# A hybrid encoder layer on one core: the experts' turn shifted into the next mixing, and the scores of the expert search taken from one merged matrix

## The reference, cut to what matters

```python
proj = rms_norm(x) @ w_in                              # 1024 -> 2592 columns
y_r  = rwkv7_group(...)                                # recurrence with a state, prompt tiles in order
y_a  = swa_group(...)                                  # window attention over 256 keys
x    = x + concat(y_r, y_a) @ w_out
t    = rms_norm(x)
q    = (t @ w_q).reshape(T, 8, 2, 128)                 # 2048 columns
s1   = q[:, :, 0] @ key1.T;  s2 = q[:, :, 1] @ key2.T  # 16 blocks of 128 scores
# top 16 of each, top 16 of their sums: 8 x 16 = 128 experts for each token, gate = softmax
act  = gelu(down[expert] . t);   x = x + sum(gate * act * up[expert])
y    = rms_norm(x)
```

## Time and profile before

| | us |
|---|---|
| median of 3 runs | 4369.31 (4369.14 to 4375.14) |
| the profiled execution | 4367.83 |
| its span in the trace | 4365.9 |
| `project` | 0 to 335 |
| sample tile | 335 to 645 |
| eight turns | 645 to 4030, 422 each |
| experts of the last tile alone | 4030 to 4366 |

### The profile page before, as it was taken

The page is one execution under the profiler, slowest core; times in us unless marked ns, Lnnn a source line. Parts: engine busy times, 40 slices in busy tenths (PEclk is TensorE's granted clock), DMA queues, the critical chain, the costliest instruction groups (busy, mean ns, idle before and its releaser), DMA issues.

```text
span 4365.9 us, 47921 instructions
## 1 busy us (share of the span) xinstructions
PE 3366.5 (77%) x13668; PEld 1870.5 (43%) x13668; DVE 2944.6 (67%) x6184; ACT 1441.0 (33%) x4151; POOL 1366.7 (31%) x1160
## 2 busy tenths in 40 slices
PE   9996837886877697869776977787778777876656
PEld 5554534452545253526352635254435434552222
DVE  1003356758876877687767877786777687769765
ACT  1001203432443335233523352335233423342222
POOL 0000002434333334334333433343334343434443
PEclk9997668898889898979897989888878898898778
DMA  4102228989899989989998999899889988999998
GB/s 189 51 37 80 81 78 337 388 360 371 326 390 369 367 329 405 352 334 363 383 359 332 366 396 363 323 370 403 350 324 364 403 342 331 380 396 347 405 420 358
DMA packets 228898, 1410.30 MB, mean 323 GB/s; under 512 B 34211, under 2 KB 40739, under 8 KB 77654
## 3 DMA queue, kind: packets, MB, share of 16 engines
q0 software_dynamic: 165888, 1208.03, 69.9%
q1 hardware_dynamic: 60102, 181.96, 11.1%
q10 hardware_dynamic: 2592, 16.66, 0.9%
HBM read 1387.39 MB, written 20.41 MB: 322 GB/s over the span
## 4 chain that ended last, share of the span: by engine, by line
PE 31%; DVE 27%; DMA 12%; issue 9%; ACT 6%; DVEq 0%; POOL 0%; ACTq 0%; POOLq 0%; SPq 0%; PEldq 0%
PE mx_ps L1435 14%; DVE ex_rows L1462 10%; DMA ex_rows<-experts,ex_expert_c 8%; PE mx_ps L1185 4%; DMA mx_fac<-w_q 2%; PE mx_ps L1168 2%; DVE mx_pqb L1285 1%; DVE mx_fac L1286 1%; DVE mx_pqb L1283 1%; DVE ex_x2c L1472 1%; PE mx_ps L978 1%; PE mx_ps L974 1%; PE mx_ps L971 1%; ACT ex_diag L1416 1%; ACT ex_coef L1409 1%
## 5 line engine op out<-in xcount | busy, mean ns | idle before, releaser
L1397 POOL DMA_INDIRECT ex_rows<-experts,ex_expert_c x1152 | 1361.9, 1182 | 2970.3 <-PE mx_ps L1435 1339.0
L1435 PE MATMUL mx_ps<-ex_rows,ex_diag 128*128 128x512 f32 x3168 | 1772.9, 707 | 638.3 <-ACT ex_diag L1416 627.9
L1462 DVE CUSTOM_DVE_ANT_0 ex_rows<-ex_rows,ex_tnc 128x1024 f32<-128x1024 f32 x1152 | 1376.4, 1222 | 277.2 <-DMA ex_rows<-experts,ex_expert_c 255.4
L1435 PEld LDWEIGHTS mx_ps<-ex_rows,ex_diag 128*128 128x128 f32 x3168 | 662.0, 222 | 1559.2 <-issue 898.6
L1406 ACT ACTIVATE ex_coef<-ex_coef 128x1 f32<-128x1 f32 x1152 | 224.9, 202 | 1510.1 <-DVE ex_coef L1462 1508.0
L1472 DVE SCALAR_TENSOR_TENSOR ex_x2c<-ex_rows,ex_coef,ex_x2c 128x1024 f32<-128x1024 f32 x360 | 462.5, 1285 | 140.2 <-ACT ex_coef L1409 139.4
L1416 ACT ACTIVATE ex_diag<-cn_ident,ex_coef 128x128 f32<-128x128 f32 x792 | 294.5, 397 | 18.5
L260 PE MATMUL psP<-pj_w_in_sb,pj_hT 128*128 128x432 f32 x768 | 279.6, 526 | 0.0
L1409 ACT ACTIVATE ex_coef<-ex_coef,ex_gate_c 128x1 f32<-128x1 f32 x1152 | 277.1, 282 | 4.7
L229 DVE TENSOR_SCALAR pj_proj_sb<-psP,pj_rstd_a 128x432 f32<-128x432 f32 x27 | 18.0, 668 | 279.2 <-PE psP L260 244.9
L1406 ACT ACT_TABLE_LOAD x137 | 175.8, 1283 | 90.3 <-issue 55.2
(11 more groups left out here) (297 smaller groups left out, 3999.8 us busy)
## 6 DMA issues: line engine op xcount, KB each, us to landing
mx_fac<-w_q SPq DMA_DIRECT2D x54, 512.0 KB, 11.0
mx_ex<-w_out SPq DMA_DIRECT2D x36, 512.0 KB, 10.7
mx_ex<-w_q SPq DMA_DIRECT2D x36, 512.0 KB, 13.3
ex_rows<-experts,ex_expert_c POOLq DMA_INDIRECT x1152, 9.2
mx_p_cur<-w_q SPq DMA_DIRECT2D x27, 512.0 KB, 13.0
mx_xs<-w_q SPq DMA_DIRECT2D x27, 512.0 KB, 13.1
proj_rows<-pj_proj_sb ACTq DMA_DIRECT2D x9, 1296.0 KB, 4.7
mx_p_cur<-proj_rows SPq DMA_DIRECT2D x9, 1296.0 KB, 8.5
```

Source lines behind the costliest of these rows:

```text
L1397: pool.indirect_dma_start(rows[:, s % RING, :], None, A["experts"], bass.IndirectOffsetOnAxis(expert_c[:, s:s + 1], 0))\
L1435: last = pe.matmul(bank(6 + c), diag[:, n % DIAGS, :], up[:, r, c * 512:(c + 1) * 512], start=n == 0, stop=n == len(ON_PE) - 1)
L1462: dve.tensor_tensor_reduce(out=down[:, r, :], in0=down[:, r, :], in1=tnc[:, :], scale=1.0, scalar=0.0, op0=ALU.mult, op1=ALU.add, accum_ou ...
```

## The change

Five things are edited together.

1. **Written-out tiles.** The loops `Fori` over the eight turns become Python loops, so each engine's program holds all turns one after the other.
2. **The experts' turn is shifted.** The work on a tile's experts begins at mark 6 of the mixing (`BEGIN`) and ends at mark 75 (`END`), where marks 72 to 75 are marks 1 to 4 of the next mixing. A `Turn` object calls the old tile's work for marks 1 to 5 and its `finish` (final norm) at mark 6. The copies for the new tile come at mark 6 (`first`). After the last turn, `alone` works off the last tile's experts one slot a mark. `STAGES` has new numbers.
3. **Earlier loads.** `mix_sync` waits for the use of the last weight block (`w_used`) instead of `tile_end`. `mu` moves to `ex`, `k_a` to `arT`, `y_out` to `pqk`, and SyncE stores `y` between `mix_sync` and `route_sync`.
4. **One matrix of scores.** `w_sc` = `w_q` times the keys (1024 x 2048) is computed once on the device, in the first block while the samples are mixed: 32 parts of four products through one bank (`merge_tensor`), copied by ScalarE (`merge_scalar`), written to memory by SyncE (`merge_sync`). `Merge.upto` issues three parts for every two marks, up to mark 22.
5. **Routing.** PE multiplies `tn` (stationary) with 16 blocks of `w_sc` in products of 512 columns and gets the scores; two copies of 1024 columns take the place of eight of 512.

```diff
-STAGES = ((7, 13, 0.3), (16, 20, 0.5), (25, 18, 0.4), (28, 6, 0.1), (38, 20, 0.3),
-          (42, 6, 0.7), (48, 9, 0.8), (59, 17, 0.0), (67, 13, 0.0), (71, 6, 0.3))
+BEGIN, END = 6, MARKS + 4
+STAGES = ((7, 3, 0.3), (16, 21, 0.5), (25, 18, 0.4), (28, 7, 0.1), (38, 22, 0.3), (42, 7, 0.7),
+          (48, 11, 0.8), (59, 16, 0.0), (67, 12, 0.0), (71, 2, 0.3), (END, 9, 0.3))
...
+class Turn:
+    def upto(self, mark):
         while self.mark < mark:
             self.mark += 1
+            if self.ahead and self.mark < BEGIN:
+                self.ahead.upto(MARKS + self.mark)
+            if self.ahead and self.mark == BEGIN:
+                self.ahead.finish()
+            self.experts.upto(self.mark)
...
+class Merge:
+    def upto(self, mark):
+        end = max(self.done, min(32, mark * 3 // 2))
+        self.run(range(self.done, end))
+        self.done = end
...
             if not sample:
-                sp.wait_ge(tile_end.sem, tile_end.due(t, 0))
+                sp.wait_ge(w_used.sem, w_used.due(t, 0))
             sp.dma_start(p_cur[:, :], proj[bass.ds(P + src, P), :]).then_inc(p_in.sem, 16)
...
-            for g in range(4):
-                slots.upto(44 + g)
-                for j in range(4):
-                    w = weights(KC + 4 * g + j).rearrange("p (k n) -> p k n", n=P)
-                    for k in range(KC):
-                        last = pe.matmul(ps[:, 2 + g, j * P:(j + 1) * P], w[:, k, :], aT[:, k, :],
+            for side in range(2):
+                for k in range(KC):
+                    if k % 2 == 0:
+                        slots.upto(44 + (KC * side + k) // 4)
+                    w = weights(KC + KC * side + k)
+                    for n in range(2):
+                        last = pe.matmul(bank(2 + 2 * side + n), aT[:, k, :], w[:, n * 512:(n + 1) * 512],
                                          start=k == 0, stop=k == KC - 1)
                     last.then_inc(w_used.sem, 1)
...
-                for j in range(4):
-                    last = pe.matmul(ps[:, g, j * P:(j + 1) * P], s12[:, 4 * g + j, :], keysT[:, j % 2, :],
-                                     start=True, stop=True)
...
+            def merge_sync(sp):
+                for j in range(4):
+                    sp.dma_start(wqT[:, j, :], A["w_qT"][j]).then_inc(wq_in[j].sem, 16)
+                for i in range(32):
+                    j, side = i // 2, i % 2
+                    sp.wait_ge(merge_copied.sem, i + 1)
+                    sp.dma_start(A["w_sc"].rearrange("(k p) n -> p k n", p=P)[:, 4 * side:4 * side + 4, j * P:(j + 1) * P],
+                                 merged[:, i % 4, :, :]).then_inc(merge_stored[i % 4].sem, 16)
+                    if side and j + 4 < 16:
+                        sp.wait_ge(merge_out.sem, i + 1)
+                        sp.dma_start(wqT[:, j % 4, :], A["w_qT"][j + 4]).then_inc(wq_in[j % 4].sem, 16)
...
+            def merge_tensor(pe):
+                def products(parts):
+                    for i in parts:
+                        j, side = i // 2, i % 2
+                        pe.wait_ge(wq_in[j % 4].sem, 16 * (j // 4 + 1))
+                        if i:
+                            pe.wait_ge(merge_copied.sem, i)
+                        for k in range(4):
+                            at = (4 * side + k) * P
+                            last = pe.matmul(ps[:, 7, k * P:(k + 1) * P], wqT[:, j % 4, at:at + P], keysT[:, j % 2, :],
...
-                with dve.Fori(0, T) as t:
-                    slots = experts_vector(dve, t)
+                ahead = None
+                for t in range(T):
+                    experts = experts_vector(dve, t)
+                    slots = Turn(ahead, experts)
                     dve.wait_ge(tile_end.sem, tile_end.due(t + 1, 0))
                     mix_vector(dve, t + 1, m, slots)
                     route_vector(dve, t + 1, slots)
                     dve.sem_inc(tile_end.sem, 1)
-                    hand_over(dve, t + 1, slots)
-                    slots.finish()
-                experts_vector(dve, T).finish()
+                    hand_over(dve, t + 1)
+                    slots.upto(MARKS)
+                    ahead = experts
+                ahead.finish()
+                experts_vector(dve, T).alone()
```

More of the change, by code:

```diff
@@ L324, in stage_tables @@
     for s in range(SLOTS):
-        mark = min(next(m for m, n in enumerate(upto) if n > s) + ADD_LAG, MARKS)
+        mark = min(next(m for m, n in enumerate(upto) if n > s) + ADD_LAG, END)
         owed += share[mark]
@@ L357, in finish, with alone, __init__, upto @@
     def finish(self):
-        self.upto(MARKS + ADD_LAG)
+        self.upto(END + ADD_LAG)
         assert all(n == SLOTS for n in self.done)
         self.last()
+    def alone(self):
+        table = [0] * BEGIN + list(range(1, SLOTS + 1))
+        self.upto(len(table) - 1 + ADD_LAG, table)
+        self.last()
+class Turn:
+    def __init__(self, ahead, experts):
+        self.ahead, self.experts, self.mark = ahead, experts, 0
+    def upto(self, mark):
+        while self.mark < mark:
+            self.mark += 1
+            if self.ahead and self.mark < BEGIN:
[3 more added lines that the diff above has]
+            self.experts.upto(self.mark)
+class Alone:
+    def upto(self, mark):
+        pass
+class Merge:
+    def __init__(self, run):
+        self.run, self.done = run, 0
+    def upto(self, mark):
+        end = max(self.done, min(32, mark * 3 // 2))
+        self.run(range(self.done, end))
+        self.done = end
+    def finish(self):
+        assert self.done == 32
 def constants(nc, ctx):
@@ L781, in mix_vector @@
                     at += 1 if o == 0 else 0
+                    if not sample and dst is pqk and o == 0:
+                        dve.wait_ge(y_stored.sem, y_stored.due(t, 0))
                     dve.wait_ge(out.sem, out.due(t, o + 1))
@@ L1300, in sb1, with merge_scalar, copies @@
                 return own.enter_context(nc.sbuf_tensor("st_" + name, shape, F32))
+            wqT = sb1("wqT", [P, 4, D])
+            merged = sb1("merged", [P, 4, 4, P])
+            wq_in = [flag(f"wq_in{n}", 16) for n in range(4)]
+            merge_out, merge_copied = flag("merge_out"), flag("merge_copied")
+            merge_stored = [flag(f"merge_stored{n}", 16) for n in range(4)]
+            def merge_sync(sp):
[19 more added lines that the diff above has]
+                            last = pe.matmul(ps[:, 7, k * P:(k + 1) * P], wqT[:, j % 4, at:at + P], keysT[:, j % 2, :],
+                                             start=True, stop=True)
+                        last.then_inc(merge_out.sem, 1)
+                return Merge(products)
+            def merge_scalar(act):
+                def copies(parts):
+                    for i in parts:
+                        act.wait_ge(merge_out.sem, i + 1)
+                        if i >= 4:
+                            act.wait_ge(merge_stored[i % 4].sem, 16 * (i // 4))
+                        act.activation(merged[:, i % 4, :, :], ps[:, 7, :].rearrange("p (k n) -> p k n", n=P), ACT.Copy)\
+                           .then_inc(merge_copied.sem, 1)
+                return Merge(copies)
             NK = SAMPLES + 1
@@ L1337, in _ @@
                           .then_inc(s_stored.sem, 16)
+                for n in range(4):
+                    sp.wait_ge(merge_stored[n].sem, 16 * 8)
                 route_sync(sp, 0, SEQ)
@@ L1493, in last @@
                     link.close()
[L1495 removed]
+                return Experts((dots, 0), (add, ADD_LAG), first=first, last=last)
             block = own.enter_context(nc.Block())
@@ L1519, in _ @@
             def _(pool):
-                with pool.Fori(0, T + 1) as t:
+                for t in range(T + 1):
                     experts_gpsimd(pool, t)
@@ L1525, in _ @@
                 act.sem_inc(tile_end.sem, 1)
-                with act.Fori(0, T) as t:
-                    slots = experts_scalar(act, t)
+                ahead = None
+                for t in range(T):
+                    experts = experts_scalar(act, t)
+                    slots = Turn(ahead, experts)
                     mix_scalar(act, t + 1, m, slots)
@@ L1553, in _ @@
                 pe.sem_inc(tile_end.sem, 1)
-                with pe.Fori(0, T) as t:
-                    slots = experts_tensor(pe, t)
+                ahead = None
+                for t in range(T):
+                    experts = experts_tensor(pe, t)
+                    slots = Turn(ahead, experts)
                     mix_tensor(pe, t + 1, m, slots)
                     route_tensor(pe, t + 1, slots)
-                    pe.wait_ge(sco_out.sem, sco_out.due(t + 1, 4))
+                    pe.wait_ge(sco_out.sem, sco_out.due(t + 1, 2))
                     pe.sem_inc(tile_end.sem, 1)
-                    slots.finish()
-                experts_tensor(pe, T).finish()
+                    slots.upto(MARKS)
+                    ahead = experts
+                ahead.finish()
```

(2 more changed lines are left out.)

130 lines of the change are left out of this document (66 added, 64 removed).

## The result

The changed kernel takes 4424.23 us (median of 4 runs, 4412.57 to 4430.02) against 4369.23 us before (4 runs). The ratio is 1.0107, with a 95% interval from 1.0081 to 1.0133: slower by 1.1%, where 4277 us and a gain of 2% were forecast. The time lies outside the range.

A forecast was written before the change was run, and what follows sets the result against it. Prediction: turns mostly bound by bytes, two stages before them by chains. Eight turns at −18.7 us (−150), sample tile +49 and once +9 give −92 from 4367.8, forecast 4277 us, range 4185 to 4375.

The forecast's parts named there:

- the clock: At a turn's end and the next mixing's head: TensorE's granted clock partly recovers, −3 us a turn, bounds 0 and −6.
- The loops: At the end of a turn: the loop's way back on VectorE disappears, 6.0 us a turn.
- The table: Slots over the marks: −7.5 and −3.0 us a turn for slots taken away, +9.5 for seven added to marks 8 to 48.
- The gap: At the turn: VectorE's 6.0 us way back and 4.9 us wait for PE go, −10.9 a turn, bounds −14 and −6.
- The loads: Next tile's loads by SyncE start earlier, counted at 0 us a turn, bounds −3 and +9.
- Once: First turn without old slots and norm −13 us, last stretch with nine more rows +22, together +9.
- Merging: Building the merged score matrix costs +49 us in the sample tile; the shorter score chain gives −3.8 in each tile.
- A: Rival, chance 0.07: bytes bound throughout, moved slots cost all of 17.5 us, +1.3 a turn, 4437 us.
- C: Rival, chance 0.07: merging in the sample tile costs +107 us instead of +49, turns gain 10 each, 4401 us.
- E: Rival, chance 0.05: nothing visible moves, the turn's gains go into the full stretch and the merging, about 4369 us.
- D: Rival, chance 0.03: a weight block costs by its weight loads, not columns; −21 us once in the sample tile, 4256 us.
- B: Rival, chance 0.20: turns close up to the bytes at some 395 us, merging mostly hidden (+28), 4190 us.

The follow-up runs named there:

- begin1: Changed kernel without merged scores, with the old slot table and the old tile ended at the next mixing's first mark; ratio 0.9871 to the kernel before.
- turn_table_back: Changed kernel without merged scores and with the seven slots taken out of marks 8 to 48 again; ratio 0.9939 to the kernel before.
- unroll: Kernel before with only the loops over the tiles written out; ratio 0.9828 to the kernel before.
- merge_late: Kernel before with written-out loops and merged scores, merging started at the sample tile's fourth mark instead of the first; ratio 0.9876 to the kernel before.
- half_scores: Kernel before with written-out loops and merged scores, half of every merged block left unloaded, same engine work; ratio 0.9709 to the kernel before.
- slots_less: Kernel before with written-out loops and merged scores, seven slots moved from marks 8 to 48 into 49 to 71; ratio 1.0059 to the kernel before.
- ring7: Kernel before with written-out loops and merged scores, seven row buffers in place of eight; ratio 1.0092 to the kernel before.

## Why the prediction was wrong

The ladder, in us of 4369 and in us of a steady turn:

| step | time | a turn | forecast a turn |
|---|---|---|---|
| loops written out | -75 | -8.9 | -6.0 |
| loads moved | +17 | +2.4 | 0 |
| hand-over behind the norm (`begin1`) | +2 | +1.6 | |
| end of the tile at mark 6 | +30 | +1.1 | -4.9, and -3 for the clock |
| slot table | +59 | +8.0 | -1.0 |
| merging | +15 | -3.9 | -3.8 |
| whole change | +47 | +0.3 | -18.7 |

Each single step is uncertain by 13 to 21 us of time; the first and the fifth are far beyond that, the fourth is beyond its own 19. The column "a turn" is of one execution each.

The turn missed its forecast by 19.0 us. Two steps of the prediction failed, by 9.0 us a turn each: the price of the slots moved into marks 8 to 48, and the gain from the end of the tile inside the next mixing. The moved loads and the hand-over make 4.0 more, and the loops gave 2.9 back.

*The loops.* The mechanism was right: 5.9 us behind MAX8, where 6.0 were forecast. The term was too small by the 3.0 us ahead of it. The change got its largest gain here.

*The table* failed in one term. The prediction put seven slots into marks 8 to 48 at +9.5, the bytes' 17.5 less half of a slack of 16 us, and gave −10.5 for the seven taken from elsewhere. Two of those seven stand ahead of MAX8, so by its own prices five slots more ahead of MAX8 should have cost 6.5 and five fewer behind it given 7.5. Measured: +15.1 and −7.1. So 1.5 us for a slot taken away was about right (1.4), and the seven cost some 18 (an estimate: 15.1 and two more at 1.4 each), the full 17.5 and not 9.5. In the frame of the kernel before, six slots more cost 21.2, above the bound of 17.5. The slack read off the DMA share (0.98 and 393 GB/s in the earlier trace rows) was not usable: with more slots the share of the stretch stayed at 0.90 to 0.91.

*The gap.* Both of VectorE's waits at the turn went, as listed: the norm's from 43.8 to 5.0, the 6 us to none. But only the loop's 6.0 came back as time. The 4.9 for the norm's wait and the 3 for the clock did not: the step measured +1.1. The sentence that failed is "Their cost stays in the sum at its old size", of the norm and the copies (about 6 us of VectorE). In the mixing they and the new tile's first additions stand ahead of TensorE's transposes (L972), and the way there grew by 14.2 us, from 40.7 in `begin1` to 54.9 in `turn_table_back`; that is as much as the 14.0 us which the turn lost behind MAX8. The gathers' pause too came back (12.42 in `unroll`, 18.79 in the kernel after). That a turn is set by the time in which rows are not asked for, and not by VectorE's idle time, at which the forecast looked, is my reading and not shown. TensorE in the kernel after:
```profile
1580.13 5.65 PE L1523 MATMUL mx_ps<-ex_rows,ex_diag 128*128 128x512 f32 x8 [13.38 <-ACT ex_diag L1506]
1585.61 1.91 PE L972 MATMUL mx_ps<-cn_ident,mx_fac 128*128 128x128 f32 x16
```
It stands still for 13.38 us ahead of these additions. Of the clock's −3 nothing is seen: the granted clock of a turn is 0.88 in both.

*The loads* were counted at 0 with bounds −3 and +9 a turn; 2.4 lies inside. The new place of the hand-over was not priced at all; it measured +1.6.

*Once:* −13 in the first turn and +22 in the tail were forecast; `turn_table_back` against `begin1` shows −16 and +30. The signs were right and the sizes near, and it was no more than a small part of the sum.

*Merging.* −3.8 a turn was right (−3.9 in both pairs of the changed kernel, −4.6 on `unroll`, −1.0 on the kernel before). In the sample tile +49 was too much: 27 to 32. `lora` moved by 15.9 where 17.5 was said, but `merge_late`, in which it does not move, ends the sample tile at most 10 us sooner, so not all of it is in the path. By its own bound (25) the sample tile is not wrong. One sum in it is: by its own terms a part takes at least 1.0 + 0.60 + 2 × 0.26 = 2.1 us and not 1.9, so 31 parts at least 66 us and not 59; the 35 taken into the path do not hang on it.

*The rivals.* A, with 0.07, came nearest: 4437 against 4424, +1.3 a turn against +0.3. Its full 17.5 for the seven slots and its nothing for the clock were right, though the queues did not fill. That its sum is so near is partly luck: it counted the 4.9 us of the norm's wait as gained, which did not come, and the moved loads at +9, where they cost 2.4. C falls by the sample tile, which grew by 27 to 32 and not by 107, and E by the ratio, whose interval leaves out 1. D, by which a block with a quarter of the weight loads is shorter, falls by 1.72 us for the new block against 1.78. B and the forecast fall by the turn of 422 us; the line drawn was 415. The rule of the Trainium skill that stood beside D (TensorE: Matmul & The Clock Gate, section Back-to-back issue gap) would have the new block at 0.40 of the old one's time; the trace shows 0.97.

What stays open: why a steady turn cannot use the 9% of the queues' time that stays free. `half_scores` (half of the bytes' price), `slots_less` (0.4 us for a slot) and `ring7` (11.8 us for a buffer) say that neither the bytes nor the number of slots alone set it. That the ring's reach over the mixing's waits does is a reading that fits all three, but only `ring7` tests it. For the same reason it stays open why an added slot costs its full price while the queues are at 0.90.

## What to carry to other kernels

A table that spreads work over the marks of another chain has to be moved one way and the other before a new one is believed: here seven of 128 slots cost 2.5 to 2.7% in either direction. Free time in a share averaged over a stage is not slack that the next piece of work can have. Work that is moved costs what it costs at its new place: here the end of a tile freed 14.0 us where it left and cost 15.2 us where it came to stand, ahead of TensorE's transposes in the mixing. And where several edits come together, time the dullest by itself: the loops written out gave all of the gain, 1.7%, and the rest of the change took it back and more.

## What was not expected of the hardware

A loop that stands on five engines costs 8.9 us a turn, though VectorE shows 6.0 at its way back. With the merged matrix read as rows of 4 KB out of every 8 KB a turn is no longer than with whole blocks of 512 KB (408.4 and 409.7 us). Bytes moved in a steady turn are the same to 0.5% in all kernels but one (152.5 MB; rate by length of the turn), so the kernels differ mainly in the time in which the queues are not busy: 34 us a turn before, 25 in `unroll`, 38 after. These are estimates from the shares of the windows below over six turns; a share is given to a hundredth, so each is good to 2 us. Before:
```profile
1092.80:3624.30 2531.50, 1982.16 (x8190) 1104.60 (x8190) 1922.51 (x4051) 957.33 (x2742) 905.60 (x768) 0.87 0.92 362
```
`unroll`:
```profile
1088.50:3565.60 2477.10, 1960.91 (x8190) 1093.33 (x8190) 1921.23 (x4051) 946.36 (x2742) 905.00 (x768) 0.89 0.94 369
```
after:
```profile
1109.80:3642.90 2533.10, 1899.73 (x6798) 949.20 (x6798) 1939.55 (x4063) 923.79 (x2688) 887.44 (x768) 0.88 0.91 361
```
